# Tile 0 first at the hand-over between sublayers, a fourth weight place and one pass for two norms, in a single-core two-block transformer kernel

## Chip, core and metric

The kernel runs on one core of one Trainium2 chip. The metric is the device time of one execution in microseconds. The kernel before was run three times: 1804.09, 1809.89 and 1814.42 us.

## The reference, cut to what matters

256 tokens of width 1024 pass two layers of a first block (feed-forward, token mixing, feed-forward, each with its own modulation of an RMS norm), a final norm with a weight, and one hybrid layer that starts with an RMS norm of its own and ends in a mixture of experts.

```python
def modulate(x, shift, scale):
    return rms_norm(x) * (1 + scale[:, None, :]) + shift[:, None, :]

def swiglu(u, w_gate, w_up, w_down):
    return (jax.nn.silu(u @ w_gate) * (u @ w_up)) @ w_down

    for l in range(DEPTH):                     # first_block, DEPTH = 2
        mod = c_act @ w_ada[l] + b_ada[l]
        sh1, sc1, g1, sh2, sc2, g2, sh3, sc3, g3 = jnp.split(mod, N_MOD, axis=-1)
        x = x + 0.5 * g1[:, None, :] * swiglu(modulate(x, sh1, sc1), ffn1_gate[l], ffn1_up[l], ffn1_down[l])
        x = x + g2[:, None, :] * token_mix(modulate(x, sh2, sc2), ...)
        x = x + 0.5 * g3[:, None, :] * swiglu(modulate(x, sh3, sc3), ffn2_gate[l], ffn2_up[l], ffn2_down[l])
    return rms_norm(x) * final_norm

    h = modulate_2(x, norm1_w, shift1, scale1) # hybrid_layer: rmsnorm(x, w) * (1 + scale) + shift
    proj = h @ w_in
    ...
```

## The kernel before

The tokens lie in two tiles of 128. All weights are float32; a product is done in three matmuls on numbers split in a rounded part and a remainder: hi*hi, lo*hi and hi*lo (`mm3`, lines 1958 to 1962). Weights come from one long stream in units of three blocks of 128 x 2048. A block lands in one of three places of `raw` (SP issues, lines 438 to 442), ACT rounds it to `w_hi` in two halves (L529), and VectorE subtracts to `w_lo` (L1032). Each of the three places of `w_hi`/`w_lo` is free again once TensorE has passed it (semaphores `used`). SP loads a block once the block before it in that place is split (`split_done`).

A feed-forward sublayer has 11 units of 256 hidden columns. Blocks 0 and 1 of a unit are gate and up (48 matmuls, `gate_up`), block 2 is down (24 matmuls, `down`), which runs one unit behind. `ACC` (banks 0 to 3) holds the sum of the sublayer: two tiles by two halves of 512. `GU` holds gate and up, `HT` the turned hidden values, split into `hT_hi` and `hT_lo`, which lie in `r_arena`. In the last unit `finish` puts the down product of the unit before in the middle of gate and up, and the last `down` goes tile by tile.

The token mixing ends in a merge of three units (`merge`): the product of the second attention, then y turned to `yT` and multiplied with the output matrix, both tiles for k 0 to 3 (`u1`), then tile and half by k 4 to 7 (`u2`).

Behind each sublayer x is updated (`gated` multiplies the sum with the gate, `added` adds it), then comes the norm: ACT squares with a sum (L553), VectorE adds the two halves (L1045), ACT takes the root (L557), VectorE inverts (L1050), ACT or VectorE scales x to `xn` (L567, L1056), TensorE turns it (`turn_x`, L1990), ACT and VectorE shift and scale the odd and even chunks to `uTf` (L575, L1105), and split them into `uT_hi` (L581) and `uT_lo` (L1113). `restart` waits for the first half of x, runs matmuls on zeros (`keep_warm`, L1950) and turns tile 0. The next sublayer's first unit is `first_columns` (mixing and hybrid: steps k of 768 columns) or `gate_up_behind` (feed-forward). Ahead of the hybrid layer the final norm with its weight is done first and the hybrid layer's norm behind it (lines 822 to 832 and 1629 to 1648).

The modulation is read in pairs of columns: POOL loads 1 MB (L497) into one of two slots, VectorE multiplies with the row of c and sums (`ada_pair`, L1064), pairs 0 to 3 (`gate_pair`), two per unit in the loop (`stage_pair`), and 20 to 23 late. Every engine runs its instructions in the order of the program, and waits on semaphores.

## Time and profile before

| | |
|---|---|
| median of three runs | 1809.89 us |
| profiled execution | 1811.05 us |
| its span, first to last instruction | 1809.2 us |
| mean granted TensorE clock | 0.981 |
| TensorE busy | 1714.7 us (95%), 8557 matmuls |
| VectorE busy | 1364.4 us (75%) |
| ACT busy | 976.1 us (54%) |
| read from HBM | 435.36 MB, 241 GB/s over the span |

Busy time counts an engine that has work in hand; for TensorE this takes in the matmuls on zeros. The granted clock is the share of the full 2.4 GHz. Idle time is given in brackets in front of an instruction, with what released it.

### The profile page before, as it was taken

What the parts mean: (1) busy time and instruction counts of PE and PEld (TensorE: products, weight loads), DVE (VectorE), ACT (ScalarE), POOL (GpSimd) and SP (SyncE); (2) the same over time, 40 slices, a digit from 0 to 9 for tenths busy, and PEclk for the clock granted to TensorE, in tenths of its full rate; (3) what the DMA queues carried; (4) which work ended last, traced back from release to release, by engine and by line L of the source; (5) the groups of instructions that cost most, each with busy time, mean ns of one, the idle gap of its engine ahead of it and who ended that gap; (6) DMA issues with size and microseconds to landing.
All of it is one profiled execution on the core that took longest, in us unless ns stands there. A gap on an engine that the chain in (4) does not pass through costs nothing.

```text
span 1809.2 us, 24914 instructions
## 1 busy us (share of the span) xinstructions
PE 1714.7 (95%) x8557; PEld 1405.4 (78%) x8557; DVE 1364.4 (75%) x2111; ACT 976.1 (54%) x1531; POOL 47.0 (3%) x92
## 2 busy tenths in 40 slices
PE   6999989999999989998989999999799998999998
PEld 4878768787788868887878877888587876888886
DVE  7787767767776678777577587876577588999997
ACT  5434454564644464445447555444445557777775
POOL 0000000000000000000000000000000000000000
PEclk9999999999999999999899999999999999999999
DMA  8988844225576748886522347987284443999994
GB/s 344 368 322 327 316 162 149 70 94 202 207 288 248 265 160 333 328 310 236 209 94 94 117 163 273 349 325 278 86 326 162 186 163 126 383 354 368 360 356 166
DMA packets 61802, 437.42 MB, mean 242 GB/s; under 512 B 6816, under 2 KB 7328, under 8 KB 9504
## 3 DMA queue, kind: packets, MB, share of 16 engines
q1 hardware_dynamic: 47360, 338.44, 50.0%
q0 software_dynamic: 12672, 92.28, 13.7%
q10 hardware_dynamic: 1696, 5.72, 0.8%
q8 instruction: 46, 0.75, 0.2%
q14 instruction: 28, 0.23, 0.0%
HBM read 435.36 MB, written 1.05 MB: 241 GB/s over the span
## 4 chain that ended last, share of the span: by engine, by line
PE 81%; DVE 11%; ACT 4%; DMA 2%; issue 2%; SPq 0%; DVEq 0%; ACTq 0%; POOLq 0%
PE bank L1960 24%; PE bank L1962 23%; PE bank L1961 23%; DVE w_lo L1032 3%; PE bank L2244 2%; DVE ada_w L1064 2%; PE bank L2262 1%; DMA arena<-ada_pairs 1%; PE bank L2096 1%; DMA ada_w<-ada_pairs 1%; PE bank L1990 1%; PE bank L2224 1%; ACT w_hi L529 1%; DVE arena L1105 1%; ACT uT_hi L581 1%
## 5 line engine op out<-in xcount | busy, mean ns | idle before, releaser
L1032 DVE TENSOR_TENSOR w_lo<-raw,w_hi 128x1024 fp32r<-128x1024 f32 x410 | 483.0, 1221 | 179.6 <-ACT w_hi L529 178.5
L529 ACT ACTIVATE w_hi<-raw 128x1024 fp32r<-128x1024 f32 x418 | 418.8, 1053 | 340.2 <-PE bank L1962 334.3
L1960 PE MATMUL bank<-w_hi,uT_hi 128*128 128x512 f32 (+2 forms) x1408 | 559.3, 397 | 44.8 <-DVE uT_lo L1113 13.4
L1961 PE MATMUL bank<-w_lo,uT_hi 128*128 128x512 f32 (+2 forms) x1408 | 544.5, 387 | 0.0
L1962 PE MATMUL bank<-w_hi,uT_lo 128*128 128x512 f32 (+2 forms) x1408 | 544.3, 387 | 0.0
L1960 PEld LDWEIGHTS bank<-w_hi,uT_hi 128*128 128x128 f32 x1408 | 271.8, 193 | 106.1 <-issue 15.0
L1962 PEld LDWEIGHTS bank<-w_hi,uT_lo 128*128 128x128 f32 x1408 | 270.7, 192 | 53.3
L1961 PEld LDWEIGHTS bank<-w_lo,uT_hi 128*128 128x128 f32 x1408 | 272.2, 193 | 47.8
L1960 PE MATMUL bank<-w_hi,r_arena 128*128 128x512 f32 (+1 forms) x744 | 293.5, 394 | 5.2 <-DVE r_arena L1858 2.5
L1962 PE MATMUL bank<-w_hi,r_arena 128*128 128x512 f32 (+1 forms) x744 | 288.9, 388 | 0.0
L1961 PE MATMUL bank<-w_lo,r_arena 128*128 128x512 f32 (+1 forms) x744 | 288.5, 388 | 0.0
L1064 DVE CUSTOM_DVE_ANT_0 ada_w<-ada_w,cmpw 128x1024 f32<-128x1024 f32 x176 | 207.1, 1220 | 8.3 <-DMA ada_w<-ada_pairs 8.2
L1960 PEld LDWEIGHTS bank<-w_hi,r_arena 128*128 128x128 f32 x744 | 139.7, 188 | 35.6 <-DVE r_arena L1858 3.3
L1962 PEld LDWEIGHTS bank<-w_hi,r_arena 128*128 128x128 f32 x744 | 139.6, 188 | 28.5
L1961 PEld LDWEIGHTS bank<-w_lo,r_arena 128*128 128x128 f32 x744 | 139.8, 188 | 26.8
L1039 DVE TENSOR_TENSOR w_lo<-raw,w_hi 128x1024 fp32r<-128x1024 f32 x94 | 110.9, 1222 | 8.4 <-ACT w_hi L544 6.9
L544 ACT ACTIVATE w_hi<-raw 128x1024 fp32r<-128x1024 f32 x94 | 94.3, 1054 | 13.7 <-PE bank L1962 13.7
L616 ACT ACTIVATE arena<-bank 128x256 f32<-128x256 f32 x88 | 33.8, 385 | 120.4 <-PE bank L1962 120.3
L497 POOL DMA_DIRECT2D ada_w<-ada_pairs x88 | 46.8, 532 | 1305.1 <-DVE mods_gate L1064 557.9
L1151 DVE TENSOR_TENSOR arena<-arena,bank 128x256 f32<-128x256 f32 x88 | 35.7, 420 | 54.5 <-ACT arena L616 54.3
L1039 DVE TENSOR_TENSOR w_lo<-ada_w,w_hi 128x1024 fp32r<-128x1024 f32 x60 | 70.6, 1222 | 4.3 <-ACT w_hi L544 3.7
L544 ACT ACTIVATE w_hi<-ada_w 128x1024 fp32r<-128x1024 f32 x64 | 64.1, 1055 | 7.2 <-PE bank L1962 7.2
(342 smaller groups left out, 1476.2 us busy)
## 6 DMA issues: line engine op xcount, KB each, us to landing
raw<-weight_stream SPq DMA_DIRECT2D x216, 1024.0 KB, 5.0
ada_w<-ada_pairs POOLq DMA_DIRECT2D x88, 1024.0 KB, 5.2
raw<-expert_blocks SPq DMA_DIRECT2D x48, 1024.0 KB, 4.9
ada_w<-expert_blocks SPq DMA_DIRECT2D x32, 1024.0 KB, 4.9
cmpw<-expert_blocks SPq DMA_DIRECT2D x16, 1024.0 KB, 4.9
arena<-ada_pairs SPq DMA_DIRECT2D x5, 1024.0 KB, 13.5
ada_w<-ada_pairs SPq DMA_DIRECT2D x3, 1024.0 KB, 13.3
cmpw<-compress_w ACTq DMA_DIRECT2D x2, 1024.0 KB, 8.5
```

Of the source, the lines that this page charges most:

```text
L497: pool.dma_start(ada_w[:, slot], ada[g]).then_inc(ada_landed[slot], 16)
L529: act.activation(w_hi[:, b], v, ACT.Copy).then_inc(hi_done, 1)
L544: act.activation(w_hi[:, b], v, ACT.Copy).then_inc(hi_done, 1)
L616: act.activation(act_g[:, t], banks[t][:, 0:F_UNIT], ACT.Silu).then_inc(silu_done, 1)
L1032: V.tensor_tensor(w_lo[:, b], v, f32(w_hi[:, b]), ALU.subtract).then_inc(split_done, 1)
L1039: V.tensor_tensor(w_lo[:, b], v, f32(w_hi[:, b]), ALU.subtract).then_inc(split_done, 1)
L1064: e = V.tensor_tensor_reduce(w[:, i], w[:, i], c, 1.0, 0.0, ALU.mult, ALU.add, dst[:, i:i + 1])
L1151: V.tensor_tensor(hid[:, t], act_g[:, t], banks[t][:, F_UNIT:2 * F_UNIT], ALU.mult).then_inc(h_done, 1)
L1960: pe.matmul(dst, xh, w_hi[:, off:off + n], start=first, stop=False, skip_group_check=True)
L1961: pe.matmul(dst, xh, w_lo[:, off:off + n], start=False, stop=False, skip_group_check=True)
L1962: return pe.matmul(dst, xl, w_hi[:, off:off + n], start=False, stop=last, skip_group_check=True)
L2244: m = pe.matmul(HT[:, a * DH:(a + 1) * DH], pT[j % 2][:, kt, a], v, start=kt == 0, stop=kt == qt, skip_group_check=True)
```

## The change

- Feed-forward tail. The last unit's gate and up run tile by tile. `last_downs` then finishes tile 0 (down products of the last two units), and then tile 1; before tile 1's last half it turns tile 0's `xn`. `finish`, `restart` and their matmuls on zeros go.
- A fourth weight place, `extra_hi` and `extra_lo`, in `r_arena`. `hT` moves to the arena, and the last unit has its own `hL`. The third block of an FFN's last unit and the last quarter of the merge's output matrix are rounded into it.
- Next blocks early. Both first blocks of the unit behind an FFN are split ahead of the norm, the third behind tile 0. FFN 2 begins in places 1 and 2 (`early_block`, `behind_gap`), which needs blocks in another order in the stream; as many are loaded as before.
- Merge. Tile 0 runs all eight k, then tile 1.
- Norm order. Tile 0's norm is done ahead of tile 1's update; tile 1's transposes move from k = 4 (or behind k 3 of tile 0) to k = 6. Tile 0 is scaled by VectorE behind an FFN too, tile 1 by ACT.
- Hybrid. z = x times the final weight, its squares and those of x give one root for the hybrid norm (`final_norm`); x itself is scaled later by ACT (`final_rows`).
- Modulation. In FFN 1's loop `stage_pair(i, 0)` stands behind the hidden product; pairs 20 and 21 are read in the mixing stage; POOL's first load waits for unit 0's third block to land and no longer for four rounded blocks.

```diff
@@ places
+        hT_hi, hT_lo = rounded("hT_hi", arena_at, 4096, 2, S), rounded("hT_lo", arena_at, 4608, 2, S)
+        hL_hi, hL_lo = rounded("hL_hi", arena_at, 5120, 2, S), rounded("hL_lo", arena_at, 5632, 2, S)
+        extra_hi, extra_lo = r_arena[:, 0:BLK], r_arena[:, BLK:2 * BLK]
@@ POOL
-                    pool.wait_ge(hi_done, 4 * HALVES)
+                    pool.wait_ge(landed[2], 16)
@@ ACT, FFN tail
-                h_split(f0 + n - 2)
-                split(u0 + n, (0,), LAST_BEHIND)
-                split(u0 + n - 1, (2,), LAST_UNIT)
+                h_split(f - 1)
+                extra_block(2, u * 16 + 16)
                 beside()
+                silu(u, f, (0,))
                 gate_out(stage, 1, SPARE)
-                f = f0 + n - 1
-                silu(u0 + n - 1, f, (0,))
+                split(u + 1, (0,))
                 h_tile(0, (hL_psum, f // FFN_UNITS + 1), hL_hi_done)
-                silu(u0 + n - 1, f, (1,))
-                split(u0 + n, (1,))
+                silu(u, f, (1,))
+                split(u + 1, (1,))
                 h_tile(1, (hT_psum, f + 1), hT_hi_done)
@@ VectorE, norms
             def norm_behind_ffn(stage, q, n, done, third=lambda i: None):
...
+                norm_tile(q, 0)
+                gated(stage, 1, 0, done)
+                shifted(n, 0)
+                remainder(n, 0, (0, 1))
+                added(1, 0)
+                x_half(stage, 1, 1, done)
+                remainder(n, 0, (2, 3))
+                third(0)
+                rms_sum(q, 1)
+                rms_inverse(q, 1)
+                third(1)
+                shifted(n, 1)
+                remainder(n, 1, range(4))
...
             def norm_behind_merge(stage, q, n, done, first=lambda i: None, second=lambda i: None):
...
                 norm_tile(q, 0)
+                for i in range(HALVES):
+                    first(i)
+                shifted(n, 0)
+                remainder(n, 0, range(4))
                 x_half(stage, 1, 0, done)
+                x_half(stage, 1, 1, done)
+                second(0)
+                rms_sum(q, 1)
+                rms_inverse(q, 1)
+                second(1)
...
+            def final_norm(stage, q, n, done, third):
+
+                for h in range(2):
+                    x_half(stage, 0, h, done)
+                    final_z(q, 0, h)
+                final_inverse(q, 0)
+                dve.wait_ge(rstd_done, 2 * q + 1)
+                for h in range(2):
+                    c = slice(h * 512, (h + 1) * 512)
+                    V.tensor_scalar(xn[:, 0, c], z[:, 0, c], rstd[:, 0:1], None, ALU.mult).then_inc(xn_done, 1)
+                x_half(stage, 1, 0, done)
+                final_z(q, 1, 0)
+                shifted(n, 0)
...
@@ VectorE, FFN tail
             def last_unit(u, f):
-                split(u, (2,), LAST_UNIT)
+                extra_block(u, 2)
                 hidden(f, (0,))
+                split(u + 1, (0,))
                 h_tile(0, (hL_hi_done, f // FFN_UNITS + 1), hL_ready)
                 hidden(f, (1,))
+                split(u + 1, (1,))
+                h_tile(1, (hT_hi_done, f + 1), hT_ready)
@@ VectorE, FFN 1 loop and mixing stage
-                    stage_pair(i, 0)
                     split(u0 + i + 1, (0,), LAST_BEHIND)
                     hidden(f0 + i)
+                    stage_pair(i, 0)
+                    split(u0 + i + 1, (1,), LAST_BEHIND)
                     stage_pair(i, 1)
-                    split(u0 + i + 1, (1,), LAST_BEHIND)
...
-                for j in (22, 23):
+                for j in range(20, 24):
                     ada_pair(pair_place(l, "ffn1", j), mods[:, 2 * j - 8:2 * j - 6])
@@ TensorE, first unit behind a norm
-                        if (t, k) == (0, 4):
+                        if (t, k) == (0, 6):
                             turn_x(n, q, 1)
...
-                        mm3(bank[t][:, :], uT_hi[:, k, tok(t)], uT_lo[:, k, tok(t)], off, 512, k == 0, k == KD - 1)
-                        if (t, k) == (0, 0):
-                            pe.wait_ge(x_ready, 4 * q + 4)
+                        mm3(bank[2 * t][:, :], uT_hi[:, k, tok(t)], uT_lo[:, k, tok(t)], off, 512, k == 0, k == KD - 1)
@@ TensorE, FFN tail
+            def last_downs(u, f, turn_first):
+
+                pe.wait_ge(hT_ready, f)
+                need(u - 1, set(), 2 * BLK, BLK, LAST_BEHIND)
+                for t in range(T):
+                    for c in range(2):
+                        for h in range(2):
+                            m = mm3(ACC[2 * t + h][:, :], hT_hi[:, c, tok(t)], hT_lo[:, c, tok(t)], 2 * BLK + c * D + h * 512, 512, False, False)
+                    if t == 0:
+                        pe.wait_ge(hL_ready, f // FFN_UNITS + 1)
+                        turn_tile(f, 1, hT_psum)
+                        need(u, set(), 2 * BLK, BLK, LAST_UNIT)
+                    else:
+                        m.then_inc(used[2], 2)
+                        pe.wait_ge(hT_ready, f + 1)
+                    for h in range(2):
+                        if (t, h) == (1, 1):
+                            turn_first()
+                        for c in range(2):
+                            m = mm3_extra(ACC[2 * t + h][:, :], hL_hi[:, c, tok(t)], hL_lo[:, c, tok(t)], c * D + h * 512, c == 1)
+                        m.then_inc(extra_used if (t, h) == (1, 1) else first_tile, 1)
...
+                gate_up(u, order=BY_TILE, at_={(0, 1): second_gate, (KD - 1, 1): last_turn})
+                last_downs(u, f, turn_first)
@@ TensorE, merge
+                for k in range(KD):
+                    if k == 3:
+                        turn_y(m, 1)
+                    for h in range(2):
+                        e = product(0, k, h)
...
+                for k in range(4):
+                    for h in range(2):
+                        e = product(1, k, h)
...
+                turn_first()
+                for h in range(2):
                     for k in range(4, KD):
...
+                        e = product(1, k, h)
...
@@ TensorE, hybrid
-            for h in (1, 2):
-                pe.wait_ge(x_ready, 4 * n6 + 2 * h)
-                keep_warm(7, ACC[0][:, :])
-            restart(n6, n6 + 1, 7)
             first_columns(u, n6, n6 + 1)
```

## Rows read from the trace of the kernel before

**Rows 1.** Busy time by stretches; columns as in the first line.

```profile
core 0: us, PE busy (x) PEld busy (x) DVE busy (x) ACT busy (x) POOL busy (x), PEclk, DMA share, GB/s
30.00:50.00 20.00, 17.82 (x79) 12.31 (x78) 16.64 (x27) 12.49 (x18) 1.19 (x2) 1.00 0.75 283
93.00:102.00 9.00, 5.34 (x17) 4.05 (x16) 9.00 (x16) 2.60 (x3) 1.06 (x2) 0.64 0.70 266
217.30:250.50 33.20, 24.17 (x110) 18.66 (x109) 18.56 (x39) 16.27 (x37) 0.00 (x0) 0.90 0.48 188
456.60:472.00 15.40, 11.13 (x40) 8.23 (x39) 10.62 (x24) 13.19 (x26) 0.00 (x0) 0.78 0.41 135
653.00:672.00 19.00, 14.62 (x67) 10.73 (x67) 15.61 (x34) 11.96 (x29) 1.06 (x2) 1.00 0.26 93
672.00:839.80 167.80, 167.80 (x765) 138.89 (x763) 133.43 (x186) 73.95 (x93) 10.60 (x20) 1.00 0.86 320
839.80:874.50 34.70, 26.70 (x106) 20.80 (x105) 18.64 (x39) 16.27 (x37) 0.00 (x0) 0.75 0.40 156
1276.70:1305.00 28.30, 18.68 (x84) 13.22 (x84) 18.17 (x40) 14.42 (x39) 0.00 (x0) 0.88 0.23 78
```

**Rows 2.** TensorE in time, FFN 1 to mixing, layer 0: start, duration, idle before.

```profile
225.13 0.39 PE L1962 MATMUL bank<-w_hi,r_arena 128*128 128x512 f32 x1
225.36 1.47 PE L1950 MATMUL bank<-zeros 128*128 128x512 bf16 x6
226.70 1.27 PE L1990 MATMUL bank<-cst,arena 128*128 128x128 f32 x8
229.81 0.47 PE L1960 MATMUL bank<-w_hi,uT_hi 128*128 128x512 f32 x1 [1.85 <-DVE uT_lo L1113]
...
235.18 0.52 PE L1960 MATMUL bank<-w_hi,uT_hi 128*128 128x512 f32 x1 [3.02 <-DVE w_lo L1095]
...
244.47 0.50 PE L1960 MATMUL bank<-w_hi,uT_hi 128*128 128x512 f32 x1 [3.44 <-DVE w_lo L1032]
```

**Rows 3.** VectorE and ACT in time, tile 0's norm; the last behind the hybrid merge.

```profile
222.85 0.69 DVE L1178 TENSOR_TENSOR arena<-bank,gate_bc 128x512 f32<-128x512 f32 x1
...
225.92 1.34 ACT L567 ACTIVATE arena<-x,stat 128x512 f32<-128x512 f32 x2 [0.38 <-DVE stat L1050]
...
1486.97 0.88 DVE L1056 TENSOR_SCALAR arena<-x,stat 128x512 f32<-128x512 f32 x2
```

**Rows 4.** TensorE in time: layer 0's merge, FFN 2's start, layer 1's FFN 1.

```profile
439.49 0.50 PE L1960 MATMUL bank<-w_hi,uT_hi 128*128 128x512 f32 x1 [0.77 <-DVE uT_lo L1342]
...
462.52 1.09 PE L1990 MATMUL bank<-cst,arena 128*128 128x128 f32 x8 [1.90 <-DVE arena L1056]
465.37 0.79 PE L1960 MATMUL bank<-w_hi,uT_hi 128*128 128x512 f32 x1 [1.76 <-DVE uT_lo L1113]
465.96 0.63 PE L1961 MATMUL bank<-w_lo,uT_hi 128*128 128x512 f32 x1
466.39 0.63 PE L1962 MATMUL bank<-w_hi,uT_lo 128*128 128x512 f32 x1
...
671.62 0.50 PE L1960 MATMUL bank<-w_hi,uT_hi 128*128 128x512 f32 x1 [1.27 <-DVE w_lo L1032]
```

**Rows 5.** TensorE in time, ahead of the hybrid layer: matmuls on zeros.

```profile
1279.60 3.20 PE L1950 MATMUL bank<-zeros 128*128 128x512 bf16 x14 [1.19 <-DVE x L1183]
```

**Rows 6.** ACT in time, behind the norm of FFN 2 in layer 1.

```profile
1091.05 1.28 ACT L819 ACT_TABLE_LOAD   x1
...
1094.26 1.99 ACT L529 ACTIVATE w_hi<-raw 128x1024 fp32r<-128x1024 f32 x2
```

**Rows 7.** VectorE and TensorE in time, mixing stage of layer 0.

```profile
270.45 4.64 DVE L1032 TENSOR_TENSOR w_lo<-raw,w_hi 128x1024 fp32r<-128x1024 f32 x4 [0.82 <-ACT w_hi L529]
...
275.49 0.45 PE L1960 MATMUL bank<-w_hi,uT_hi 128*128 128x440 f32 x1
```

**Rows 8.** VectorE in time, FFN 1 of layer 0.

```profile
91.87 1.23 DVE L1064 CUSTOM_DVE_ANT_0 ada_w<-ada_w,cmpw 128x1024 f32<-128x1024 f32 x1 [2.40 <-DMA ada_w<-ada_pairs]
```

More of the change, by code:

```diff
@@ L1345, in merge @@
                         split(u0 + 1, (2,))
-                split(u0 + 2, (1,))
+                extra_block(u0 + 2, 1)
                 following()
-                split(u0 + 2, (2,))
-                norm_behind_merge(stage, q, n, (used[1], u0 + 4), between)
+                norm_behind_merge(stage, q, n, (extra_used, stage + 1), first, second)
             def job_bias(j0, jobs, j):
```

426 lines of the change are left out of this document (217 added, 209 removed).

## The prediction

> **What bounds the kernel now.** I read the busy time by stretches first. From 672 to 840 us TensorE is busy for all of 167.80 us at full clock, with VectorE at 133.43 and the DMA engines at a share of 0.86 [rows 1]. So in the body of the FFN a unit costs what its matmuls cost, and no edit there can win anything. The time that can be won lies at the places where one sublayer hands to the next, since there TensorE waits for a norm. I call them A (FFN 1 to mixing, layer 0), B (merge to FFN 2, layer 0), C (FFN 2 to FFN 1 of layer 1), D and E (A and B again in layer 1), F (FFN 2 of layer 1 to the hybrid block) and G (hybrid merge to the experts), and the start of the kernel.
>
> For each I count three things from its stretch: the length less PE busy; the clock loss, which is (1 - granted clock) times PE busy; and the matmuls on zeros that keep TensorE busy (six per restart in A, C and D, 0.21 us each, 1.3 us; in F these 14 and 7 ahead of them, 4.5 us) [rows 1, 2, 5].
> - A: 33.20 - 24.17 = 9.0, plus 0.10 x 24.17 = 2.4, plus 1.3: 12.7 us.
> - B: 4.3 + 2.4 = 6.7. E repeats it: 6.7.
> - C: 4.4 + 0 + 1.3 = 5.7.
> - D: 8.0 + 6.7 + 1.3 = 16.0.
> - F: 9.6 + 2.2 + 4.5 = 16.3.
> - start (93 to 102 us): 3.7 + 1.9 = 5.6.
> In all 69.7 us. To it I add the wait of 0.77 us at tile 1's first product of the merge, three times, 2.3 us [rows 4]. The pool is 72.0 us.
>
> Then I read TensorE's instructions in A with what released each [rows 2]: zeros until 226.70, eight transposes, 1.85 us until the first uT_lo, 3.02 us until a half of block 1 of the next unit is split, 3.44 us until block 2 is. Two kinds of loss: the norm itself, and weight blocks that are split late because VectorE does them between parts of the norm.
>
> **The change, part by part.** All matmuls are kept; one of 512 columns starts every 0.23 us [rows 2].
>
> *Tail of an FFN (A, C, D, F).* Before, tile 0's sums close with 12 matmuls left, 2.7 us. After, tile 0 closes with both units' products, and behind it stand tile 1's 12 products of the unit before and 6 of the last: 18 x 0.227 = 4.1 us before the transposes of tile 0, and 6 more (1.4 us) behind them. The chain it must cover: from the gating multiply of tile 0's second half at 222.85 to the start of scaling at 225.92 is 3.1 us; scaled on VectorE (0.88 for two halves, as the merge does) xn is there after 3.5 and 3.9 us [rows 3]. That is under 4.1 plus the end of a matmul, so the wait and the zeros go. From the start of the transposes to the first uT_lo product there were 229.81 - 226.70 = 3.1 us [rows 2]; 1.1 are the transposes, 1.4 now six matmuls, and 0.65 stays. The fourth place (the 4096 columns of r_arena) is what lets the last unit's third block be rounded early, so both blocks 0 and 1 of the next unit are split before the norm. Its cost is no instruction more; ACT and VectorE do the same halves in another order. Block 2 of the next unit is split behind tile 0 (two halves of 1.16 us [rows 7]); a step k of the first mixing product has 1.02 us of matmuls, so k = 5, which needs it, comes 5.1 us after the start, while VectorE is through after some 4.3. The waits of 3.02 and 3.44 us go; tile 1's transposes move from k = 4 to k = 6 and find xn ready. A and D: 0.65 left.
>
> *Modulation pairs 20 and 21* leave that tail and are read in the mixing stage, four in a row in place of two: 4 x 1.15 = 4.6 us more on VectorE ahead of the latent norm, for which ACT waits in order, with the split of the block behind it. That block's first half is split from 270.45 on; TensorE wants it at 275.49 [rows 7]. Moved by 4.6 it ends at 276.2: 0.75 us of stall, in A and D. Bounds: nothing, if VectorE comes earlier to the pairs, to 4.6 us. I take 0.75, from the two rows. A and D then keep 1.4 each.
>
> *C.* Steps of gate and up last 0.68 us, so tile 1's transposes at k = 6 come 4.1 us after the start: they wait about 0.55, tile 1's first product 0.5. The wait of 1.27 us for the next unit's first block behind two modulation pairs [rows 4] stays and grows to about 2.1, since TensorE arrives earlier and VectorE doesn't. C keeps 0.65 + 0.55 + 0.5 + 2.1 = 3.8.
>
> *Merge (B, E, G).* Tile 0 runs all eight k, then tile 1. Tile 1's first k comes 24 matmuls later, so its wait of 0.77 goes [rows 4]; the last quarter block lies in the fourth place, which is free once the pb product has read r_arena. Tile 0's norm has 24 matmuls (5.4 us) of cover before the transposes and 24 behind; the block that FFN 2 begins with is split in that time. Left: 0.1 at tile 1's transposes, 0.5 at its first product. New: ACT loads a table and runs two SiLUs of the condition rows (1091.05 to 1094.26, 3.2 us) and then the next block [rows 6]; TensorE now arrives about 8 us earlier, and that block is late by some 1.4 us. B and E keep 2.0 each. G gains only its 0.77, already counted: VectorE gets a third split in front of tile 0's shift, so x(1,1) is ready when it was.
>
> *F.* Two norms become one: z = x times the final weight, its squares with those of x, one root per tile with its own eps. That takes away 21 zeros and two rounds of squares, root and reciprocal [rows 5]. But z adds 0.7 us per half on VectorE: the chain is 0.7 us for each of two halves and 0.5 of small sums longer, so 1.6 us of wait stays before tile 0's transposes. And x(1,0) with its z (2.1 us) stands ahead of tile 0's shift, which costs 2.0 at the first product. 0.4 further on: F keeps 4.0; the trace has no such step, so from 2 (z hidden behind the squares) to 7 us (all of its operations in line). ACT's last scale of x (four halves, 2.7 us) ends before the next unit's block is wanted.
>
> *Start.* Two things hit the stall at 93 us. The first two modulation loads are issued when unit 0's third block has landed in place of at 45 us, into a stretch where the DMA share is 0.75 [rows 1]; and in the loop the wait for a pair (2.40 us, [rows 8]) no longer stands ahead of the split and the hidden product. The second is enough: 0 left, 5.6 gained. If the loads delay weights instead, up to 2 us of the gain is lost. The Trainium skill (DMA: Bandwidth & Descriptors, Issuing engines are not separate DMA queues) says that transfers of all issuers run on the same 16 engines and interleave, so that an earlier start only shifts who waits; by it the early loads bring nothing, and the sum would stand as it is, on the new order alone. No run here has shown which holds.
>
> *The sum.* Left: 1.4 + 2.0 + 3.8 + 1.4 + 2.0 + 4.0 = 14.6, and 3.0 for a clock that falls once or twice yet (B's 2.4 is the nearest row). Gain 72.0 - 17.6 = 54.4. The profiled execution took 1811.05 us, so 1756.6; the median of the runs is 1.2 below it: about 1756.
>
> **Rivals.**
> 1. *The clock stays down.* For: in B, idle time of 1.90 and 1.76 us with only eight transposes between was followed by matmuls 0.43 us apart, at 0.78 over the stretch [rows 1, 4]; the zeros that stood before the transposes in A, C and D are taken out, and short waits remain at five places. Against: C, with waits of 1.3 to 1.9 us, kept 1.00. Price: B's 2.4 at six places is 14.4, 11 more than I took: 1767; D's 6.7 at six places is 40, 37 more: 1793. The middle is about 1775. The Trainium skill (TensorE: Matmul & The Clock Gate, What's actually happening, and Part 4: PE-mode transpose) says that the throttled state is the default and only activity lifts it, and that transposes don't count as that; by it this rival would be the likelier outcome wherever a wait stands beside the eight transposes. C speaks against it.
> 2. *The chains are longer than their cover.* In an FFN tail VectorE now has three blocks, two hidden products and two turned tiles to finish before it may gate tile 0; I found 0.1 us to spare. If that slips by 2 us in four tails, 8 us are lost: 1764. It lies in the forecast's range.
> 3. *Slower: modulation pairs hold the FFN 1 loop.* With stage_pair(i, 0) now between the hidden product and the split of block 1, a pair that lands late holds a block that TensorE wants within the same unit. Counted from the moment block 0's place is free (24 matmuls into a unit of 16.9 us), VectorE ends the split of block 0 at 3.5 us, the hidden products at 7.0, the pair at 9.3 and block 1 at 11.6; TensorE wants block 1 at 16.9, which is 5.3 us of slack, and the pair's load, issued 7.6 us before the count starts, has until 7.0 to land. It decides once a pair lands more than 5.3 us behind its turn (the longest wait now is 2.40 us, [rows 8]). At 9.2 us behind, 3.9 us are lost in each of 16 units, 63 us, and the time is 1820. DMA share 0.86 is for it, VectorE at 133 of 168 against [rows 1].
> 4. *It changes little.* The next late thing at each place (the fourth place, pairs, table loads) takes 80% of the gain: 1800.
>
> **How the numbers follow.** Forecast (with rival 2) 1738 to 1768: 0.65. Rival 1, 1768 to 1793: 0.20. More gain, below 1738: 0.04. Rival 4, around 1800: 0.07, of which I put 0.04 within 0.5% of before. Rival 3: 0.04. The range 1738 to 1785 holds the forecast and most of rival 1. A measurement of this kernel tells about 0.5% from no change, 9 us: faster 0.92, same 0.04, slower 0.04.
>
> **What would show it.** PE idle in A's stretch falls from 9.0 to under 2.5 us, no wait on w_lo between the FFN's last product and the mixing product, no zeros there; B's two waits of 1.9 and 1.8 are gone and one before the next unit's first block appears; F shows one round of roots per tile and about 4 us of idle; at 93 us there is no gap. A clock under 0.9 in three or more of these stretches would be rival 1. The prediction fails if the idle time comes back in the stages that I take as untouched.

## The result and the profile after

The changed kernel takes 1761.2 us (median of four runs, 1760.2 to 1763.4) against 1811.7 us before: a ratio of 0.973, 95% interval 0.970 to 0.976, or 50 us less. The forecast was 1756.0 us, range 1738 to 1785. The profiled execution of the changed kernel has a span of 1761.7 us, 47.5 less than before, and its granted clock is 0.992 in place of 0.981.

I read it stretch by stretch, as [rows 1] was read. Busy time by stretches of the kernel after: the start, A, the block behind A's latent norm (the norm inside the mixing stage), B (two stretches), C, D, the block behind D's, E, F and G.

```profile
core 0: us, PE busy (x) PEld busy (x) DVE busy (x) ACT busy (x) POOL busy (x), PEclk, DMA share, GB/s
60.00:115.00 55.00, 55.00 (x252) 45.55 (x251) 49.95 (x74) 23.98 (x30) 5.28 (x10) 1.00 0.96 367
205.00:232.00 27.00, 25.76 (x135) 21.39 (x134) 19.98 (x39) 18.21 (x39) 0.00 (x0) 1.00 0.58 238
255.00:270.00 15.00, 10.48 (x49) 9.45 (x48) 11.26 (x20) 8.87 (x12) 0.53 (x1) 0.89 0.81 300
442.00:458.00 16.00, 14.65 (x66) 11.21 (x65) 10.24 (x19) 12.70 (x22) 0.00 (x0) 1.00 0.29 92
470.00:493.00 23.00, 21.19 (x98) 17.04 (x97) 20.32 (x31) 9.66 (x12) 1.58 (x3) 1.00 0.84 315
624.00:651.00 27.00, 24.52 (x113) 19.08 (x112) 21.89 (x47) 18.30 (x39) 1.06 (x2) 1.00 0.33 127
811.00:838.00 27.00, 26.17 (x139) 21.77 (x138) 20.00 (x39) 17.71 (x39) 0.00 (x0) 1.00 0.52 193
860.00:875.00 15.00, 10.09 (x41) 8.97 (x40) 11.75 (x20) 8.86 (x12) 0.53 (x1) 0.77 0.81 290
1066.00:1104.00 38.00, 34.64 (x158) 28.17 (x157) 32.62 (x49) 18.12 (x23) 3.17 (x6) 1.00 0.90 341
1234.00:1262.00 28.00, 25.14 (x136) 21.08 (x135) 22.02 (x48) 21.15 (x49) 0.00 (x0) 1.00 0.32 113
1426.00:1460.03 34.03, 28.02 (x146) 20.65 (x146) 21.17 (x62) 20.23 (x40) 0.00 (x0) 0.95 0.19 70
```

Length less PE busy is the idle time: 0 at the start, 1.2 us in A, 0.8 in D, 2.9 in F, 2.5 in C. The granted clock is 1.00 in all of them, where A had 0.90, D 0.75 and F 0.88 before. The two rows that stand out are 255:270 and 860:875: 4.5 and 4.9 us idle at a clock of 0.89 and 0.77. The kernel before had no idle time at all at the same work.

TensorE in A, after the change (answers to [rows 2]; start, duration, and in brackets the idle time before with its releaser): no zeros, eight transposes between two groups of tile 1's products, and 0.80 and 0.45 us of wait where 1.85, 3.02 and 3.44 stood.

```profile
216.87 0.39 PE L2052 MATMUL bank<-r_arena,hL_lo 128*128 128x512 f32 x1
218.06 1.10 PE L2080 MATMUL bank<-cst,arena 128*128 128x128 f32 x8 [0.80 <-DVE arena L1109]
...
220.15 0.40 PE L2052 MATMUL bank<-r_arena,hL_lo 128*128 128x512 f32 x1
221.00 0.47 PE L2043 MATMUL bank<-w_hi,uT_hi 128*128 128x512 f32 x1 [0.45 <-DVE uT_lo L1182]
```

The clearest account comes from instructions that both traces have: the start of the same instruction before and after, and how much the difference grew since the row above. What the prediction expected of each stretch stands beside it (pool less what it left there). NSA jobs are the steps of one of the two attentions of the token mixing, hybrid jobs those of the attention in the hybrid layer.

```
stretch, up to this instruction            before     after    gained  expected
1st unit's turned tiles, layer 0            59.82     60.40     -0.6      0
4th unit's turned tiles (start)            116.51    110.82      6.3      5.6
transposes in the NSA jobs, layer 0 (A)    329.67    315.36      8.6     11.3
3rd unit of FFN 2, layer 0 (B)             509.93    491.34      4.3      5.5
2nd unit of FFN 1, layer 1 (C)             688.57    665.90      4.1      1.9
transposes at 1016, layer 1 (D)           1016.20    987.24      6.3     14.6
3rd unit of FFN 2, layer 1 (E)            1134.84   1102.87      3.0      5.5
first product behind F (F)                1313.66   1266.09     15.6     12.3
last hybrid job                           1430.78   1381.60      1.6      0
first gather of the experts (G)           1507.62   1460.03     -1.6      0.8
end (spans)                               1809.2    1761.7      -0.1      0
clock, not placed                                                        -3.0
sum                                                             47.5     54.5
```

The forecast total came out and two of its terms did not: D fell short by 8 us and A by 3, in the main at the block behind the latent norm, and F and C gave 3.3 and 2.2 us more.

These rows hold the clock of one execution before and one after, and that is partly chance. The 1.6 us of the hybrid jobs show it: nothing was changed there and the idle time is the same, but TensorE ran for a while at the lower level before and not after.

```profile
1420.00:1440.00 20.00, 19.51 (x101) 16.27 (x101) 10.86 (x21) 12.80 (x27) 0.00 (x0) 0.91 0.63 242
1266.00:1382.00 116.00, 115.44 (x624) 95.21 (x623) 89.15 (x137) 62.86 (x97) 3.17 (x6) 1.00 0.56 210
```

The first row is of the kernel before, around the last of its hybrid jobs: (1 - 0.91) x 19.51 = 1.8 us of clock. The second is of the kernel after, all of its hybrid jobs.

### The profile page after: what moved, and what is told of

Same layout as the page of the kernel before. It is cut to its first block, busy times and chain, and to the rows that moved or that the text cites. A ratio compares the mean times of both kernels' runs of the same rounds, so it can differ in the third digit from the quotient of the medians.

```text
span 1761.7 us, 24830 instructions
## 1 busy us (share of the span) xinstructions
PE 1688.8 (96%) x8511; PEld 1391.1 (79%) x8518; DVE 1361.5 (77%) x2106; ACT 981.9 (56%) x1540; POOL 46.8 (3%) x92
## 4 chain that ended last, share of the span: by engine, by line
PE 78%; DVE 11%; DMA 5%; ACT 3%; issue 3%; SPq 0%; DVEq 0%; ACTq 0%; POOLq 0%
PE bank L2043 23%; PE bank L2045 22%; PE bank L2044 22%; DVE w_lo L1085 3%; DVE ada_w L1117 2%; DMA raw<-weight_stream 2%; PE bank L2342 2%; DMA ada_w<-ada_pairs 1%; PE bank L2360 1%; DMA arena<-ada_pairs 1%; ACT w_hi L531 1%; PE bank L2172 1%; PE bank L2322 1%; PE bank L2080 1%; DVE arena L1174 1%
## 5 line engine op out<-in xcount | busy, mean ns | idle before, releaser
L2043 PE MATMUL bank<-w_hi,uT_hi 128*128 128x512 f32 (+1 forms) x1384 | 543.1, 392 | 26.6 <-DVE w_lo L1085 11.0
L2044 PE MATMUL bank<-w_lo,uT_hi 128*128 128x512 f32 (+1 forms) x1384 | 530.0, 383 | 0.0
L2045 PE MATMUL bank<-w_hi,uT_lo 128*128 128x512 f32 (+1 forms) x1384 | 529.6, 383 | 0.0
L2043 PEld LDWEIGHTS bank<-w_hi,uT_hi 128*128 128x128 f32 x1384 | 262.8, 190 | 84.6 <-issue 17.7
L2043 PE MATMUL bank<-w_hi,r_arena 128*128 128x512 f32 (+1 forms) x392 | 155.9, 398 | 4.2 <-DVE r_arena L1940 2.5
L2045 PE MATMUL bank<-w_hi,r_arena 128*128 128x512 f32 (+1 forms) x392 | 152.0, 388 | 0.0
L2044 PE MATMUL bank<-w_lo,r_arena 128*128 128x512 f32 (+1 forms) x392 | 151.7, 387 | 0.0
L2043 PE MATMUL bank<-w_hi,hT_hi 128*128 128x512 f32 x320 | 124.7, 390 | 0.2 <-DVE w_lo L1085 0.2
L2045 PE MATMUL bank<-w_hi,hT_lo 128*128 128x512 f32 x320 | 124.8, 390 | 0.0
L2044 PE MATMUL bank<-w_lo,hT_hi 128*128 128x512 f32 x320 | 124.7, 390 | 0.0
L2043 PEld LDWEIGHTS bank<-w_hi,r_arena 128*128 128x128 f32 x392 | 73.7, 188 | 19.4 <-DVE r_arena L1940 3.3
L2045 PEld LDWEIGHTS bank<-w_hi,r_arena 128*128 128x128 f32 x392 | 73.6, 188 | 14.7
L2044 PEld LDWEIGHTS bank<-w_lo,r_arena 128*128 128x128 f32 x392 | 73.8, 188 | 13.3
```

The lines of the kernel that those rows point to most:

```text
L2043: pe.matmul(dst, xh, hi, start=first, stop=False, skip_group_check=True)
L2044: pe.matmul(dst, xh, lo, start=False, stop=False, skip_group_check=True)
L2045: return pe.matmul(dst, xl, hi, start=False, stop=last, skip_group_check=True)
```

## The experiments

Line numbers in the fences are those of each kernel; all times are compared with runs of the kernel before on the same chip. For effects of a few microseconds the stretch in the trace decides, not the median, and there the wait more than the clock: each kernel has one trace, and a loss of 1.4 to 1.8 us of clock at one place comes and goes between traces of the same code (last section).

**Pairs 20 and 21 ahead of the splits (e1).** First the stall itself. VectorE, then TensorE, of the kernel after, in the mixing stage of layer 0:

```profile
247.19 1.22 DVE L1117 CUSTOM_DVE_ANT_0 ada_w<-ada_w,cmpw 128x1024 f32<-128x1024 f32 x1
...
251.68 1.23 DVE L1117 CUSTOM_DVE_ANT_0 ada_w<-ada_w,cmpw 128x1024 f32<-128x1024 f32 x1 [3.26 <-DMA ada_w<-ada_pairs]
...
254.47 1.23 DVE L1117 CUSTOM_DVE_ANT_0 ada_w<-ada_w,cmpw 128x1024 f32<-128x1024 f32 x1 [0.42 <-DMA ada_w<-ada_pairs]
...
259.85 4.63 DVE L1085 TENSOR_TENSOR w_lo<-raw,w_hi 128x1024 fp32r<-128x1024 f32 x4 [0.81 <-ACT w_hi L531]
```

```profile
256.07 0.63 PE L2117 MATMUL bank<-cst,modf 128*128 128x128 f32 x4
261.22 0.44 PE L2043 MATMUL bank<-w_hi,uT_hi 128*128 128x440 f32 x1 [4.52 <-DVE w_lo L1085]
```

Two pairs are read at once (247.19 is the last half of the second); the third has to wait 3.26 us for its load, the fourth 0.42, since only two places hold pairs and a place is filled again only when it has been read. The first pair was through at 246.1; 5.2 us is the median from issue to landing of a pair's load on the page, and 251.3 is when the third could be there.

```diff
+                for j in (20, 21):
+                    ada_pair(pair_place(l, "ffn1", j), mods[:, 2 * j - 8:2 * j - 6])
                 split(u_mix + 1, (0, 1))
...
-                for j in range(20, 24):
+                for j in (22, 23):
```

> The changed kernel, with modulation pairs 20 and 21 read on VectorE before it splits the blocks of the second mixing unit, in place of behind them (22 and 23 stay). Theory 1: the stall of 4.52 us (layer 0) and 4.92 us (layer 1) at the block behind the latent norm comes from four pairs in a row, two of which find their load not landed (3.26 and 0.42 us of wait), since only two places hold pairs. VectorE had 3.12 us idle ahead of those splits, so the 4.6 us of the two pairs cost nothing there; both stalls go to 0, and with them the slower matmuls behind (5.5 and 6.2 us over the nominal pace in the two stretches, where the kernel before had none): 12 to 14 us, about 1748. Rival: it is ACT's order (root, table load, then the split) that is late whatever VectorE does; over 2 us of stall stay in each layer: 1756 or more.

Measured: 1749.9 us, ratio 0.966 (0.964 to 0.968). Both stalls are gone and the clock with them. Busy time by stretches, the work of 255:270 and 860:875 in this kernel:

```profile
252.00:267.00 15.00, 15.00 (x85) 13.78 (x84) 7.75 (x8) 6.28 (x9) 0.00 (x0) 1.00 0.80 304
848.00:863.00 15.00, 15.00 (x85) 13.60 (x84) 9.41 (x14) 8.92 (x12) 0.53 (x1) 1.00 0.85 329
```

Theory 1 holds. From the first product behind A's and D's norm to the attention behind the stall (221.00 to 278.22 and 826.08 to 884.98 us in the kernel after), e1 is 6.3 and 8.0 us shorter: 9.4 us of wait and 4.8 of clock. The slower matmuls are thus 4.8 us in all, not the 5.5 and 6.2 of the expectation. The span is 12.5 us shorter, since a wait for a pair's load at E was longer in this execution:

```profile
1088.65 0.78 PE L2174 MATMUL bank<-cst,arena 128*128 128x128 f32 x4 [3.52 <-DVE arena L1264]
```

That wait, 2.49 us in the kernel after, is nobody's doing in e1: with the order at E untouched it is 3.89, 3.37, 3.28, 3.44 and 5.46 us in e3, e4, e7, e8 and e9, and 1.45 in e2. Spans therefore differ by a few microseconds for this wait alone.

**The pairs in the tail, as before (e2).**

```diff
                 gate(stage + 1, mods[:, 16:24])
+                for j in (20, 21):
+                    pair(j, mods[:, 2 * j - 8:2 * j - 6])
                 last_unit(u0 + n - 1, f0 + n - 1)
```

> The changed kernel, with pairs 20 and 21 read where the kernel before reads them, in the tail of FFN 1 behind the gate's modulation and ahead of the last unit's blocks. The stalls of 4.52 and 4.92 us in the mixing stage go, as in the run before. Theory 1: the tail has no room for 4.6 us more on VectorE; its idle times there are 2.21 and 1.93 us, so TensorE waits about 2 us for the hidden product of tile 0 and 1 to 3 us more for tile 0's norm, in each layer: 1752 to 1758. Rival: the move out of the tail was not needed and costs only: 1748, as the run before.

Measured: 1767.7 us, ratio 0.977 (0.975 to 0.979), 18 us more than e1 with the same pairs elsewhere. Neither expectation had the size: TensorE waits 6.65 us in layer 0 and 6.57 in layer 1 at one instruction. TensorE, then VectorE, of this kernel:

```profile
206.12 0.39 PE L2047 MATMUL bank<-w_hi,uT_lo 128*128 128x512 f32 x1
213.16 0.66 PE L2180 MATMUL bank<-cst,arena 128*128 128x128 f32 x2 [6.65 <-DVE arena L1264]
```

```profile
208.03 1.23 DVE L1117 CUSTOM_DVE_ANT_0 ada_w<-ada_w,cmpw 128x1024 f32<-128x1024 f32 x1 [4.89 <-DMA ada_w<-ada_pairs]
```

The second pair of the tail is again the third in a short time, and its load is 4.89 us late. The waits make 13.2 us. Around them the clock is 0.83 in 205:225 (13.35 us busy) and 0.88 in 812:840 (20.97 us busy), 2.3 and 2.5 us more. The sum of 18.0 is the difference of the medians. The profiled execution, the fastest of the five, is only 12.5 us longer than e1's, in part for its short wait at E. So the pairs had to leave this tail; only where they went was wrong. A pair costs 2.3 us of VectorE and, if two stand just ahead of it, 3 to 5 us of waiting for its place to be filled.

**The start: late loads (e3) and old order (e4).**

```diff
-                    pool.wait_ge(landed[2], 16)
+                    pool.wait_ge(hi_done, 4 * HALVES)
```

> The changed kernel, with GpSimd starting the first modulation loads as late as the kernel before does (behind the rounding of all first blocks). Theory 1 (of the prediction): the gap at 93 us went by the new order of the FFN 1 loop alone, so nothing changes: 1761, no TensorE wait over 0.5 us between 60 and 115 us. Rival: it went by the earlier loads; then the wait for a pair is back by some 2 us and TensorE loses 3 to 6 us near 93 us: 1764 to 1767.

```diff
+                    stage_pair(i, 0)
                     split(u0 + i + 1, (0,), LAST_BEHIND)
                     hidden(f0 + i)
-                    stage_pair(i, 0)
-                    split(u0 + i + 1, (1,), LAST_BEHIND)
                     stage_pair(i, 1)
+                    split(u0 + i + 1, (1,), LAST_BEHIND)
```

> The changed kernel, with the FFN 1 loop on VectorE in the order of the kernel before (a pair, split, hidden product, a pair, split), the early loads kept. Theory 1 (of the prediction): the wait for a pair stands again ahead of the split and the hidden product, and 3 to 6 us come back near 93 us: 1764 to 1767. Rival: the early loads are enough, no gap: 1761.

Measured: 1764.2 and 1764.4 us, ratios 0.973 and 0.973: too near to the changed kernel to tell by time. The trace tells. The stretch from 60 to 115 us, in e3 and then in e4:

```profile
60.00:115.00 55.00, 55.00 (x252) 45.52 (x251) 50.33 (x74) 24.11 (x30) 5.30 (x10) 1.00 0.96 360
```

```profile
60.00:115.00 55.00, 52.27 (x229) 42.93 (x229) 48.15 (x71) 21.61 (x27) 5.27 (x10) 0.97 0.95 358
```

With the new order TensorE is busy throughout, early loads or not; e3's VectorE even waits 2.30 us for a pair and nobody is hurt. With the old order the wait is back, 2.73 us and a clock of 0.97 (1.6 us): 4.3 of the 6.3 us that the start gained. The step that put the gain on the new order holds. Both medians are 3 us above the changed kernel's; for e3 the stretch shows no cause, and its wait at E is 1.4 us longer.

**The zeros of the kernel before (e5).**

```diff
                 pe.wait_ge(x_ready, 4 * q + 1)
-                keep_warm(warm, ACC[0][:, :])
                 turn_x(n, q, 0)
...
                 pe.wait_ge(x_ready, 4 * n6 + 2 * h)
-                keep_warm(7, ACC[0][:, :])
```

> The kernel before, without the matmuls on zeros ahead of tile 0's transposes at A, C, D and F (3 x 6 and 7 + 7 + 7). They ran while TensorE waited for the norm. Theory 1 (rival 1 of the prediction, the clock): without them the clock falls beside the eight transposes, at A, C, D and F by 2.4 to 6.7 us each: 1820 or more. Theory 2: the clock doesn't depend on them here; the same wait stands where they stood: 1808 to 1813, and the granted clock of the four stretches stays within 0.03 of that of the kernel before.

Measured: 1809.3 us, ratio 0.998 (0.996 to 1.000): no loss, and a gain of at most 8 us that the runs can't tell from none. The profiled execution is the fastest of twelve (1797.6 us), with a granted clock of 0.989 where the others have 0.974 to 0.984, so its clock flatters this kernel. Busy time by stretches of this kernel (span of its profiled execution: 1795.8 us) at A, around tile 0's transposes at C, at D and at F:

```profile
211.00:243.00 32.00, 21.68 (x101) 17.03 (x100) 21.84 (x44) 17.64 (x40) 0.54 (x2) 0.94 0.51 204
644.00:655.00 11.00, 6.61 (x33) 4.73 (x32) 7.55 (x21) 7.21 (x21) 0.00 (x0) 1.00 0.00 0
834.50:869.00 34.50, 25.78 (x121) 20.98 (x122) 18.16 (x40) 17.35 (x39) 0.00 (x0) 0.90 0.40 152
1262.00:1290.00 28.00, 14.06 (x63) 11.37 (x62) 18.61 (x43) 15.17 (x41) 0.00 (x0) 0.76 0.17 57
```

By time theory 2 holds. By the clock it holds for C, which stays at 1.00 with 4.4 us idle of 11 and no zeros, and A and D even read higher (0.94 and 0.90 for 0.90 and 0.75), which one lucky execution can't prove: A and D run the same code in the kernel before, and read 0.90 and 0.75. At F it doesn't: without zeros there is one wait of 7.46 us, and the clock is 0.76 in place of 0.88, (1 - 0.76) x 14.06 = 3.4 us lost for 2.2. So in these two traces the zeros bought 1 us of clock in one place, and no loss by time shows without them. What this says of my pool: 3 x 1.3 and 4.5 us of zeros are time in which TensorE waits for the norm. Taking the zeros out turns that time into idle time (1.28 us in A); to win it the norm has to come earlier.

**The hidden product first (e6).** In FFN 2, the hidden product of unit 1 goes ahead of both splits, and in the loop ahead of the pair beside it.

```diff
-                unit(1)
+                hidden(f0 + 1)
+                split(u0 + 2, (0, 1), LAST_BEHIND)
...
-                        ada_pair(places[1], mods_step[:, 2:4], c_next)
                         hidden(f0 + i)
+                        ada_pair(places[1], mods_step[:, 2:4], c_next)
```

> The changed kernel, with FFN 2's first units in another order on VectorE: the hidden product of unit 1 ahead of both splits, and in the loop the hidden product ahead of the pair that stands with it. Theory: the waits of 0.84 and 0.97 us (layer 0) and 0.87 and 2.49 us (layer 1) that TensorE has before the turned tiles come from pairs that VectorE reads, or whose load it waits for (1.90 us in layer 1), ahead of the hidden product; all four go below 0.3: 4 to 5 us, 1757. Rival: VectorE is behind as a whole in these units, and the next block split takes over the wait: under 1 us gained.

Measured: 1758.7 us, ratio 0.969 (0.966 to 0.972). Three of the four waits are gone; the fourth went from 2.49 to 1.77 us. By the waits that is 3.4 us. The median is 2.5 us under the changed kernel's, which the intervals don't tell from none, and the fourth wait differs between executions by more than it fell. For it the later run with all moves (e11) is the better evidence: it is gone there. The one that stayed has its cause in VectorE's trace of the kernel after:

```profile
1095.20 1.23 DVE L1117 CUSTOM_DVE_ANT_0 ada_w<-ada_w,cmpw 128x1024 f32<-128x1024 f32 x1 [1.90 <-DMA ada_w<-ada_pairs]
```

It is the loop's first pair, which stands ahead of split and hidden product, and whose load is late behind four gate pairs.

**The router's block behind the hybrid merge (e7, e9).** TensorE in G, kernel after:

```profile
1439.72 0.39 PE L2052 MATMUL bank<-r_arena,uT_lo 128*128 128x512 f32 x1
1442.93 1.97 PE L2117 MATMUL bank<-cst,modf 128*128 128x128 f32 x8 [2.82 <-DVE x L1299]
1445.11 3.14 PE L2032 MATMUL bank<-zeros 128*128 128x512 bf16 x11 [0.22 <-issue]
1448.09 1.04 PE L2080 MATMUL bank<-cst,arena 128*128 128x128 f32 x8
1450.97 0.28 PE L2661 MATMUL bank<-uT_hi,w_hi 128*36 128x256 f32 x1 [1.85 <-DVE uT_lo L1182]
```

From the merge's last matmul to the first gather (1460.03) it is 20.3 us; before it was 17.7. The wait in front of the gate's transposes is 2.82 us in place of 2.18, and they take 1.97 us, half pace.

```diff
-            norm_behind_merge(q6 + 2, n6 + 1, lambda: split(um + 2, (2,)), lambda: token_hi(0))
+            norm_behind_merge(q6 + 2, n6 + 1, second=lambda: token_hi(0), third=lambda: split(um + 2, (2,)))
```

> The changed kernel, with the router's block behind the hybrid merge rounded behind tile 1's root and scaling, in place of between tile 0's scaling and its shift. Theory: behind the hybrid merge (G) the change loses 2.6 us, since VectorE waits 2.06 us for ACT's rounding and splits for 2.3 us before it may update x; that pushed x(1,1) to 1442.9, the wait there to 2.82 us, and the eight transposes behind it run at half pace (1.97 us in place of 1.09). With the block later x(1,1) comes 1.5 us earlier, the wait is at most 1.5 us and the transposes take 1.1: 1.5 to 3 us gained, 1759. Rival: the block is then late for the router's product: nothing gained.

Measured: 1761.4 us, ratio 0.971 (0.968 to 0.974): the rival, by another way. x is there earlier (wait 1.51 us), the transposes take 1.09, and then the product waits 3.33 us for uT_lo, since ACT and VectorE now have the block in front of tile 1's shift.

```diff
+            norm_behind_merge(q6 + 2, n6 + 1, second=lambda: split(um + 2, (2,)), third=lambda: token_hi(0))
```

> The changed kernel, with the router's block rounded on ACT between tile 0's rounding and tile 1's squares, and split on VectorE a half on either side of tile 1's root; the plain rounding of tile 0's tokens goes behind tile 1's scaling. The run with the block behind tile 1's scaling took the wait before x(1,1) from 2.82 to 1.51 us and gave 1.5 us back at the first product of tile 1 (1.85 to 3.33 us), since ACT and VectorE then had the block in front of tile 1's shift. Theory: placed here it is in nobody's way; x(1,1) is waited for by 1.5 us, the product by 1.9 us, and G ends 2 us earlier: 1759. Rival: tile 1's squares come 1.5 us later behind it, and the transposes of tile 1 pay what was won: 1761.

Measured: 1758.1 us, ratio 0.970 (0.966 to 0.973). Its profiled execution has a span of 1773.1, longer by single waits for pair loads elsewhere (5.46 us at E), so only G is read from it:

```profile
1454.15 0.39 PE L2052 MATMUL bank<-r_arena,uT_lo 128*128 128x512 f32 x1
1456.05 1.09 PE L2117 MATMUL bank<-cst,modf 128*128 128x128 f32 x8 [1.51 <-DVE x L1299]
...
1459.57 1.04 PE L2080 MATMUL bank<-cst,arena 128*128 128x128 f32 x8
1462.45 0.28 PE L2661 MATMUL bank<-uT_hi,w_hi 128*36 128x256 f32 x1 [1.85 <-DVE uT_lo L1182]
```

From the last matmul of the merge to the router's product it is 8.3 us, against 11.25 in the kernel after, and to the first gather (1471.52) it is 17.4 us, against 20.3: 3 us, a little more than the change had lost there.

**The first pairs of layer 1 (e8).**

```diff
                     gate_pair(0)
-                    gate_pair(1)
                 split(u0 + 1, (0,), LAST_BEHIND)
                 hidden(f0, banks=ACC)
                 split(u0 + 1, (1,), LAST_BEHIND)
+                if l:
+                    gate_pair(1)
```

> The changed kernel, with the first modulation pair of layer 1's FFN 1 read behind the split of the first block and the hidden product, and the second behind the split of the next block. Theory: the wait of 1.60 us at C (649 us) is two pairs, 4.6 us, ahead of that split; the block's first half is rounded by 645.8, so the wait falls under 0.3 us: 1.5 us gained, 1760. Rival: the pairs then delay the blocks behind them and the wait comes back within the next unit: no gain.

(The expectation describes the first pair as behind the split; as the diff shows, it stayed ahead, and only the second moved.) Measured: 1762.1 us, ratio 0.971 (0.968 to 0.974), no difference by time, but the wait is gone and nothing follows it: C's stretch has 0.87 us idle where it had 2.48.

```profile
624.00:651.00 27.00, 26.13 (x121) 20.58 (x120) 20.78 (x43) 18.26 (x40) 0.53 (x1) 1.00 0.33 123
```

**One part undone: block 1 rounded late (e10).**

```diff
                 silu(u, f, (1,))
-                split(u + 1, (1,))
+                if early:
+                    split(u + 1, (1,))
...
-                norm_behind_ffn(l * 3 + 1, l * 3 + 1, lambda: split(u_mix, (2,)))
+                norm_behind_ffn(l * 3 + 1, l * 3 + 1, lambda: split(u_mix, (1,)), lambda: split(u_mix, (2,)))
```

> The changed kernel, with one part undone in FFN 1's tail (A and D): block 1 of the next unit is not rounded and split ahead of the norm, but behind tile 0's rounding, and block 2 behind tile 1's root, as in the kernel before. Tile 0 still ends wholly first. Theory: the early rounding carries its share of the gain by itself; TensorE wants block 1 2.7 us and block 2 5.5 us after its first product, VectorE ends them at 4 and 8 us: waits of 1 to 2.5 us at each, 3 to 4 us in each of A and D: 1767 to 1769. Rival: tile 0 ahead of tile 1 is all that matters, since VectorE, freed of a block in the tail, gates tile 0 earlier by as much: within 2 us of 1761.

Measured: 1774.8 us, ratio 0.978 (0.976 to 0.981), and 12.1 us more in the span. TensorE in A of this kernel (VectorE's order is changed in the same way):

```profile
219.96 0.47 PE L2047 MATMUL bank<-w_hi,uT_hi 128*128 128x512 f32 x1 [0.47 <-DVE uT_lo L1184]
...
223.94 0.49 PE L2047 MATMUL bank<-w_hi,uT_hi 128*128 128x512 f32 x1 [1.64 <-DVE w_lo L1150]
...
229.25 0.73 PE L2047 MATMUL bank<-w_hi,uT_hi 128*128 128x512 f32 x1 [1.90 <-DVE w_lo L1150]
```

The waits are as the theory has them, 3.5 us in each layer, while the 0.80 us in front of tile 0's transposes is gone: the rival was right that VectorE gates tile 0 earlier, but not by as much. The clock is 0.94 in 204:233 and 0.80 in 258:275, where the kernel after has 1.00 and 0.90. By the starts of the attention's transposes behind them (283.43 and 894.33 for 278.22 and 884.98) the two layers lose 5.2 and 4.1 us. The rest of the 12.1 lies where the edit changes nothing, at E above all, where the wait is 4.28 us in this execution. Rounding the next blocks ahead of the norm carries 9.3 of the 47.5 us, about a fifth of the whole gain.

**All moves together (e11).** e1, e6 with both of layer 1's loop pairs behind the hidden product, e8 and e9, and ACT's SiLUs of the condition rows behind the rounding of FFN 2's second block.

```diff
-                act.wait_ge(c_landed, l * 32 + 48)
-                act.activation(c_bc, c_bc, ACT.Silu).then_inc(c_ready, 1)
-                act.activation(c_next, c_next, ACT.Silu).then_inc(c_ready, 1)
...
                     behind_gap(u0)
...
+                ahead()
                 silu(u0, f0, banks=ACC, early=early)
```

> The changed kernel with the moves of this study together: pairs 20 and 21 ahead of the splits of the mixing stage (12 us), the hidden product first in FFN 2 and in layer 1 both pairs behind it (5 us; the wait of 1.77 us that stayed at E was the first pair's load, ahead of the split and the hidden product), the first pairs of layer 1's FFN 1 behind the splits (1.6 us), the router's block in the middle (up to 2 us), and ACT's two SiLUs of the condition rows behind the rounding of FFN 2's second block (the wait of 0.98 us at B and E). The places are far apart, so the gains add: 1761 - 12 - 5 - 1.6 - 2 - 2 = 1738. Rival: weights then arrive late, since the stream is asked for earlier; waits on blocks appear and half of the gain beyond the first move is lost: 1744 or more.

Measured: 1737.6 us, ratio 0.9585 (0.956 to 0.961): the 1738 that was expected, 24 us under the changed kernel, and the fastest of all. Moving the SiLUs was run only here, and so were the pairs behind the hidden product in layer 1. Busy time by stretches of this kernel, at A, B, D and E:

```profile
205.00:232.00 27.00, 25.76 (x135) 21.39 (x134) 20.10 (x40) 18.39 (x39) 0.00 (x0) 1.00 0.60 242
436.00:470.00 34.00, 33.63 (x155) 27.23 (x154) 26.11 (x39) 23.48 (x37) 1.05 (x2) 1.00 0.62 236
812.00:840.00 28.00, 27.07 (x159) 23.20 (x158) 24.61 (x44) 20.00 (x44) 1.06 (x2) 1.00 0.45 163
1030.00:1090.00 60.00, 59.64 (x272) 48.76 (x271) 49.48 (x73) 34.21 (x52) 3.17 (x6) 1.00 0.81 307
```

B and E have 0.37 us idle left each, and the long wait at E is gone. F keeps its 2.87 us and G 1.5 and 1.8.

No run undoes the order of the tiles, the order of the merge or the single norm ahead of the hybrid layer. For those parts, F's 15.6 us among them, the account rests on the waits and releasers in the traces before and after.

## Why the prediction was right, point by point

- **The pool** held as a description of where time was lost, and its loss of 72.0 us was within reach: after the change the same places keep little. Its zeros (8.4 us) were rightly counted: taken out alone they gain nothing sure (e5), but with the norm's chain shortened their time goes too. In F's row, 15.6 us, 7.0 are idle time (9.86 before, 2.86 after) and 2.5 clock (0.91 over 27.34 us busy, 1276.70 to 1313.66, and 1.00 after), and the 6.1 that are left hold its 4.5 us of zeros. The clock entries are weaker, each one reading of one execution. The 1.6 us in the hybrid jobs, which I had taken as untouched, are such a reading and not an effect of the change.
- **Tail of an FFN.** The chain was forecast to fit with 0.1 us to spare. It missed by 0.80 us in A and 0.38 in D, and fitted in C: in A the split that stands ahead of the gating began late, because its block landed 1.67 us after ACT was ready for it (209.56 us). 0.65 for the first uT_lo product measured 0.45. Zeros and the waits of 3.02 and 3.44 us are gone as said, and e10 shows that the early rounding is what removed the latter.
- **Pairs 20 and 21** is the step that failed. I took 0.75 us with bounds of 0 and 4.6, from a chain in which VectorE only has 4.6 us more to do. It measured 4.52 and 4.92 us of wait, the second beyond my bound, and 1.7 and 3.1 us of clock behind them. Left out was the load: four pairs in a row with two places wait 3.26 + 0.42 us. With that term the same chain gives 0.75 + 3.7 = 4.4. The page of before had the number for it, 5.2 us from issue to landing of a pair; I costed the moved step's instructions and not its loads. e1 removes the stall.
- **C:** 3.8 expected, 2.5 measured. The transposes at k = 6 didn't wait (0.55 expected), the first uT_lo cost 0.47, tile 1's product 0.36, and the block 1.60 in place of 2.1. e8 confirms the cause of the last.
- **Merge.** B: 0 + 0.36 + 0.98 for 0.1 + 0.5 + 1.4, so the term for ACT's SiLUs was right in kind (e11 has it gone once they are moved). Missed were two waits further on, for the hidden product behind modulation pairs: 0.84 and 0.97 us in B, 0.87 and 2.49 in E. I had taken these units as untouched, and idle time coming back in such stages was my own sign that the prediction fails; 5.2 us of it did. It is the same kind of error as with pairs 20 and 21: TensorE arrives earlier, and the pairs and their loads don't. In G the split in front of tile 0's shift was costed at nothing; it cost 2.6 us, from the wait of 2.82, the half pace behind it, and tile 1's scaling on ACT.
- **F:** 1.6 + 2.0 expected, 1.21 + 1.65 measured, and the 0.4 further on didn't appear. The clock there went from 0.88 to 1.00.
- **Start:** 0 left, and the order did it alone (e3). From the statement of the Trainium skill (DMA: Bandwidth & Descriptors, Issuing engines are not separate DMA queues) that transfers of all issuers share the 16 engines and interleave, I had concluded that earlier loads bring nothing; with the new order e3 agrees, 0 us idle with late loads too. Whether they help under the old order is not shown: it lost 4.3 us with early loads (e4), and with late ones 6.8 in the kernel before but only 2.9 in e5, whose clock stayed at 1.00 from 60 to 115 us (52.12 us busy).
- **Clock residual,** 3.0 us: too small, and in another place. There is none in the stretches of A to F, but 1.7 and 3.1 us behind the two stalls, which I had not foreseen, and 1.4 in G.
- **Rivals.** Rival 1 didn't come: the stretches of A to F all run at 1.00, and only the two behind the stalls are under 0.9. The rule of the Trainium skill beside it (TensorE: Matmul & The Clock Gate, Part 4: PE-mode transpose), that transposes don't count as activity, would have made A, C and F slow, as each has eight of them next to a wait; the trace doesn't agree. Nor does C in e5, where they stand between waits of 1.29 and 1.85 us without zeros and the clock is 1.00; but A and D in e5, with the same two waits and longer ones behind, read 0.94 and 0.90, so the rule is not refuted everywhere. Rival 2 came in at 0.8 and 0.4 us, not 2. Rival 3: VectorE's longest wait for a pair in the FFN 1 loop with the new order is 2.30 us (e3), far under 5.3, and the loops run at the pace of their matmuls. Rival 4, a next late thing that takes the gain, is what happened, in the main in the two mixing stages: A and D lack 11 of the 72 us.

The median came within 5 us (the span within 7) since errors of both signs cancelled: A and D together 11 us short, B and E 3.7, G 2.4; F, C, the start and the hybrid jobs 7.8 better, and 3.0 that were held back for the clock (0.7 more were lost outside these places). So the closeness of the total is luck in part; that the tails, the merge and F lose their waits as said is not.

## What to carry to other kernels

When a step that reads streamed data is moved, its load moves with it: count the places that hold such data and the time from "place free" to "landed", and put no more of these steps in a row than there are places (here two; the third waited 3 to 5 us). Put them where the engine is idle anyway, and behind the product that the next engine waits for. In a hand-over, let one tile finish wholly first and round the next weights ahead of the norm. Test matmuls on zeros by leaving them out; here no loss by time showed. And read a clock loss of 1.5 us in a single trace as chance until another trace has it.

## What the runs showed of the hardware that I had not expected

A wait costs more than its length. Busy time by stretches of the kernel after, right behind the stalls of 4.52 and 4.92 us, TensorE without a gap:

```profile
261.20:275.00 13.80, 13.78 (x74) 12.78 (x76) 7.63 (x9) 7.07 (x11) 0.00 (x0) 0.88 0.62 238
866.70:880.00 13.30, 13.28 (x56) 12.27 (x57) 6.76 (x8) 5.32 (x10) 0.00 (x0) 0.77 0.65 248
```

A part of the matmuls there ran at 1.2 GHz, one start every 0.37 us in place of 0.20: (1 - 0.88) x 13.78 = 1.7 us and (1 - 0.77) x 13.28 = 3.1 us lost after the wait was over. The traces of the thirteen kernels have 21 waits of 3.97 to 7.46 us later than 50 us into the kernel; behind every one of them the next 14 us show a clock under 1.00, at a cost of 1.5 to 3.1 us.

A shorter wait may cost the same or nothing. The mixing stage has a wait of 1.57 us at one instruction, which no edit touches. Of its 26 occurrences (13 kernels, two layers) 7 were followed by a clock of 0.88 and 19 by 1.00. The kernel after has one of each, in layer 0 and in layer 1:

```profile
373.00:387.00 14.00, 13.96 (x88) 12.42 (x88) 6.21 (x12) 9.21 (x27) 0.00 (x0) 1.00 0.38 142
981.00:995.00 14.00, 13.58 (x70) 11.62 (x71) 6.75 (x14) 8.25 (x22) 0.00 (x0) 0.88 0.38 144
```

In G it is regular: the transposes of the gate take 1.75 to 1.97 us in the seven traces that have all eight in one row behind a wait of 2.82 us, and 1.09 us in the five where the wait is 2.18 or 1.51. So the size of the wait alone doesn't decide it: before the change B had 1.90 and 1.76 us and a clock of 0.78 [rows 1, 4], and E in the kernel after had 2.49 us and 1.00. What does stays open.
